# Norms and gate rows of one stage computed inside the stage before, joins by token half, modulation over seven stages

## What is computed

```python
for i in range(DEPTH):                       # 4 layers, mixers: gdn, sb, dsa, gdn
    x = x + 0.5 * swiglu(rmsnorm(x, ffn1_norm[i]), ffn1_w_gu[i], ffn1_w_down[i])
    x = x + mixer_i(rmsnorm(x, mix_norm[i]))
    x = x + 0.5 * swiglu(rmsnorm(x, ffn2_norm[i]), ffn2_w_gu[i], ffn2_w_down[i])
x = rmsnorm(x, final_norm)
...
m = split(silu(c) @ mod_w[i] + mod_b[i], 9)  # shift, scale, gate for three places
modulate(x, g, shift, scale) = rmsnorm(x, g) * (1 + scale) + shift
macaron_ffn(xs, ...) = xs + 0.5 * gate * swiglu(modulate(xs, g, shift, scale), ...)
```

## Time and profile before

| what | us |
|---|---|
| median of 3 runs | 3823.49 (3817.28 to 3826.62) |
| the profiled execution | 3812.9 |
| its span, first to last instruction | 3811.1 |
| PE busy | 3521.2 (92%) |
| DVE busy | 2263.3 (59%) |
| ACT busy | 1843.9 (48%) |
| GpSimd busy | 610.4 (16%) |
| a feed-forward stage of the first model with nothing beside it | 186.44 |

### The profile page before, as it was taken

The page is one execution under the profiler, slowest core; times in us unless marked ns, Lnnn a source line. Parts: engine busy times, 40 slices in busy tenths (PEclk is TensorE's granted clock), DMA queues, the critical chain, the costliest instruction groups (busy, mean ns, idle before and its releaser), DMA issues. The chain is left out here.

```text
span 3811.1 us, 44895 instructions
## 1 busy us (share of the span) xinstructions
PE 3521.2 (92%) x18342; PEld 2970.9 (78%) x18342; DVE 2263.3 (59%) x2508; ACT 1843.9 (48%) x2354; POOL 610.4 (16%) x208
## 2 busy tenths in 40 slices
PE   7989899999899996899999899899998799999999
PEld 6879777788788875688888778787888468787887
DVE  4566569675666667666667555545455555545654
ACT  4454356664456552456554344444443344444443
POOL 0001149571133320142401100000000000000000
PEclk9999999999999998999999999999999899999999
DMA  5532156565376752376742145454544125454453
GB/s 221 188 133 89 45 210 248 216 250 189 116 270 236 265 199 100 145 265 241 263 160 96 57 147 188 163 188 155 188 168 160 38 89 188 158 191 148 155 204 133
DMA packets 89977, 653.55 MB, mean 171 GB/s; under 512 B 10033, under 2 KB 10033, under 8 KB 10929
## 3 DMA queue, kind: packets, MB, share of 16 engines
q1 hardware_dynamic: 78768, 573.10, 41.5%
q0 software_dynamic: 11008, 77.60, 5.7%
HBM read 649.61 MB, written 1.05 MB: 171 GB/s over the span
## 5 line engine op out<-in xcount | busy, mean ns | idle before, releaser
L1562 DVE TENSOR_TENSOR w_lo<-raw,w_hi 128x2048 fp32r<-128x2048 f32 x540 | 1420.9, 2636 | 646.7 <-ACT w_hi L1080 646.4
L1080 ACT ACTIVATE w_hi<-raw 128x2048 fp32r<-128x2048 f32 x540 | 1031.2, 1913 | 592.2 <-PE acc L521 403.3
L519 PE MATMUL wrk<-w_hi,h_hi 128*128 128x512 f32 (+1 forms) x2496 | 971.2, 389 | 58.8 <-DVE w_lo L1562 37.9
L521 PE MATMUL wrk<-w_hi,h_lo 128*128 128x512 f32 (+1 forms) x2496 | 954.7, 382 | 0.0
L520 PE MATMUL wrk<-w_lo,h_hi 128*128 128x512 f32 (+1 forms) x2496 | 953.9, 382 | 0.0
L519 PEld LDWEIGHTS wrk<-w_hi,h_hi 128*128 128x128 f32 x2496 | 472.5, 189 | 155.2 <-DVE w_lo L1562 48.9
L2308 POOL TENSOR_TENSOR arena<-arena,c 128x2048 f32<-128x2048 f32 x92 | 490.7, 5342 | 472.6 <-ACT arena L1080 447.6
L521 PEld LDWEIGHTS wrk<-w_hi,h_lo 128*128 128x128 f32 x2496 | 472.2, 189 | 92.5
L520 PEld LDWEIGHTS wrk<-w_lo,h_hi 128*128 128x128 f32 x2496 | 472.8, 189 | 85.0 <-issue 0.2
L519 PE MATMUL acc<-w_hi,hid_hi 128*128 128x512 f32 x1144 | 447.4, 391 | 9.4 <-DVE hid_lo L1645 9.4
L521 PE MATMUL acc<-w_hi,hid_lo 128*128 128x512 f32 x1144 | 445.4, 389 | 0.0
(11 more groups left out here) (263 smaller groups left out, 3864.5 us busy)
## 6 DMA issues: line engine op xcount, KB each, us to landing
raw<-in_wts SPq DMA_DIRECT2D x540, 1024.0 KB, 4.8
arena<-in_mods POOLq DMA_DIRECT2D x72, 1024.0 KB, 5.2
const<-in_const SPq DMA_DIRECT2D x1, 2176.0 KB, 10.1
c<-in_bias POOLq DMA_DIRECT2D x8, 256.0 KB, 3.4
x<-in_x SPq DMA_DIRECT2D x1, 1024.0 KB, 5.3
c<-in_c SPq DMA_DIRECT2D x1, 1024.0 KB, 4.8
out<-x SPq DMA_DIRECT2D x1, 1024.0 KB, 3.9
row<-in_rows SPq DMA_DIRECT2D x1, 512.0 KB, 11.3
```

Source lines behind the costliest of these rows:

```text
L519: nc.tensor.matmul(o, l_h, r_h, start=first, stop=False, skip_group_check=True)
L521: return nc.tensor.matmul(o, l_l, r_h, start=False, stop=last, skip_group_check=True)
L1080: return nc.scalar.activation(o, i, f, **kw)
L1562: tt(w_lo[:, ns % SLOTS, :], raw[:, ns % SLOTS, :], w_hi[:, ns % SLOTS, :].bitcast(F32), ALU.subtract).then_inc(lo_ready, 1)
```

## The change

- The list of stages has `mod` inside `ffn2_3` (step 2) and `final_norm` inside `b0_ctx` (step 2): their ACT and DVE instructions are laid behind that step's.
- `AHEAD`: inside `ffn2_3`, `b0_ctx` and `b0_ffn0`, at step 4, ACT makes the statistics and DVE the normalised stream of the next stage, `b0_ctx`, `b0_ffn0` and the context part of `b0_attn` ("ready"). Each such place, and `final_norm`, has ACT load two activation tables. `stat` is doubled for it. PE turns the first two quarters of such a stage between the last `down` blocks. SP loads `c` at the start of `ffn2_3`, no longer before `b0_ctx`.
- `gate_rows` of the five feed-forward stages moves into step 6 of its own stage, `rows` into step 1 of `ffn1_0`, and again into step 1 of `ffn2_0` (the tile `c` is overwritten by `mix_0`).
- Modulation is shared by seven stages, with 14, 12, 14, 13, 13, 13 and 13 products from `ffn1_0` on.
- For a follower that needs a fresh norm ("norm"), the last `down` blocks go by token half: `turn_hid` of the last step one block earlier, both column halves of token half 0, then token half 1. Statistics and normalising of half 0 are laid beside the blocks of half 1.
- With a shift, ACT now writes the scaled and shifted quarter to `shifted` and copies it to `h_hi` in one instruction of 512 columns; DVE subtracts once.
- In the gated-delta mixer two `side` units come ahead of the wait for the squares (one in the second half), and later places have as many fewer.

The core of the diff:

```diff
+INSIDE = dict(rows="ffn2_0", mod="ffn2_3", final_norm="b0_ctx")
+AHEAD = dict(ffn2_3="b0_ctx", b0_ctx="b0_ffn0", b0_ffn0="b0_attn")
+ROWS_AT, MOD_AT, FINAL_AT, AHEAD_AT, GATE_AT = 1, 2, 2, 4, 6
+MOD_SHARE = dict(ffn1_0=7, ffn2_0=6, ffn1_1=7, ffn2_1=13, ffn1_2=13, ffn2_2=13, ffn1_3=13)
...
-                if "l" in prm:
-                    gate_rows(i, name, prm)
...
                     down(s - 1, 0, 0)
+                    if s == STEPS - 1 and not early:
+                        turn_hid(s)
                     down(s - 1, 0, 1)
                     if s == STEPS - 1:
-                        turn_hid(s)
+                        if early:
+                            turn_hid(s)
+                        else:
+                            down(s, 0, 0)
+                            down(s, 0, 1)
                     down(s - 1, 1, 0)
                     down(s - 1, 1, 1)
+                    if name in ROWS_IN and s == ROWS_AT:
+                        rows(i, name)
+                    if "l" in prm and s == GATE_AT:
+                        gate_rows(i, name, prm)
...
-                prepare(0, range(12, 16), range(16, 18), range(18, 20), range(20, 24))
+                prepare(0, range(12, 14), range(14, 17), range(17, 18), range(18, 20), range(20, 24))
...
-                prepare(1, [29], [30], [], [31])
+                prepare(1, [29], [30], [], [], [31])
...
+                    if name in AHEAD and s == AHEAD_AT:
+                        j = op_at(AHEAD[name])
+                        act.wait_ge(der_ready, 1)
+                        nc.scalar.preload_act_table_set("natural_log_exp_and_others")
+                        statistics(j, src=(c, c_new, before(j, "c")) if ops[j][0] == "attn" else None)
+                        nc.scalar.preload_act_table_set("silu_and_others")
...
-                m = fn(o, v, ACT.Copy, scale=a) if shift is None else fn(o, v, ACT.Identity, scale=a, bias=shift)
+                    if shift is None:
+                        m = fn(h_hi[:, k, tok(t)], v, ACT.Copy, scale=a)
+                    else:
+                        steps.mark(fn(shifted[:, 8 * t + k, :], v, ACT.Identity, scale=a, bias=shift))
+                if shift is not None:
+                    steps.wait()
+                    m = fn(h_hi[:, 4 * half:4 * half + 4, tok(t)], shifted[:, 8 * t + 4 * half:8 * t + 4 * half + 4, :], ACT.Copy)
```

More of the change, by code:

```diff
@@ L53, with mod_start @@
 OPS = op_list()
-MOD_OPS = ["ffn2_0", "ffn1_1", "ffn2_1", "ffn1_2", "ffn2_2", "ffn1_3"]
-MOD_PIECES = 2 * 9 * KC // 2
-MOD_EACH = MOD_PIECES // len(MOD_OPS)
+INSIDE = dict(rows="ffn2_0", mod="ffn2_3", final_norm="b0_ctx")
+AHEAD = dict(ffn2_3="b0_ctx", b0_ctx="b0_ffn0", b0_ffn0="b0_attn")
+ROWS_AT, MOD_AT, FINAL_AT, AHEAD_AT, GATE_AT = 1, 2, 2, 4, 6
+MOD_SHARE = dict(ffn1_0=7, ffn2_0=6, ffn1_1=7, ffn2_1=13, ffn1_2=13, ffn2_2=13, ffn1_3=13)
+MOD_OPS = list(MOD_SHARE)
+ROWS_IN = ("ffn1_0", "ffn2_0")
+MOD_PIECES = sum(MOD_SHARE.values())
+def mod_start(name):
+    return sum(MOD_SHARE[n] for n in MOD_OPS[:MOD_OPS.index(name)])
 CTX_CHUNKS = 5 * KC
@@ L216, in bank_uses @@
     if kind == "ffn":
-        return ["row0", "row1"] * ("l" in prm) + [f"{n}" for s in range(STEPS) for n in (f"gu{s}0", f"gu{s}1", f"t{s}")]
+        rows_at = {GATE_AT: ["row0", "row1"]} if "l" in prm else {ROWS_AT: [f"mrow{r}" for r in range(4)]} if prm["a"] in ("ffn1_norm0", "ffn2_norm0") else {}
+        return [n for s in range(STEPS) for n in [f"gu{s}0", f"gu{s}1"] + rows_at.get(s, []) + [f"t{s}"]]
     if kind == "final":
         return []
-    if kind == "rows":
-        return ["row0", "row1", "row2", "row3"]
-    if kind == "mod":
+    if kind in ("rows", "mod"):
         return []
@@ L433, in follower, with opens, op_at, stat_of @@
                 j += 1
-            ok = j < len(ops) and late(ops[j][0], ops[j][2]) and all(k not in UPDATES for k, _, _ in ops[i + 1:j])
-            return j if ok and ops[j][2]["x"] == ops[i][2]["x"] else None
+            return j if j < len(ops) else None
+        def opens(i):
+            if ops[i][1] in AHEAD.values():
+                return "ready"
+            return "late" if late(ops[i][0], ops[i][2]) else "norm"
+        def op_at(name):
+            return [k for k, o in enumerate(ops) if o[1] == name][0]
+        def stat_of(i, nth=0):
+            return stat[:, (before(i, "norm") + nth) % 2, :]
         def turned_bank(i, t, half, nth=0):
@@ L562, in turn @@
                     v = h_tok
+                    if opens(i) == "ready" and not nth:
+                        last = [k for k in range(i) if ops[k][0] in UPDATES and ops[k][1] not in INSIDE][-1]
+                        _, ready, count = stream(last)
+                        pe.wait_ge(ready, count + 2 * t + half + 1)
                 if nth:
@@ L761, in scores, with prepare @@
                     m.then_inc(filled, 1)
-                def prepare(half, first, second, third, fourth):
+                def prepare(half, ahead, first, second, third, fourth):
                     k, heads = 2 * g + half, range(half * HALF, half * HALF + HALF)
@@ L1658, in ffn @@
                         split_to(ns + 3 * s + 3)
+                    if name == "ffn2_3" and s == MOD_AT:
+                        mod()
+                    if name == "b0_ctx" and s == FINAL_AT:
+                        j = op_at("final_norm")
+                        final(j, *ops[j][1:])
+                    if name in AHEAD and s == AHEAD_AT:
+                        j = op_at(AHEAD[name])
+                        normalise(j, src=(c,) if ops[j][0] == "attn" else None)
                 hid_low(STEPS - 1)
```

239 lines of the change are left out of this document (135 added, 104 removed).

## The result

| what | before | after |
|---|---|---|
| median | 3820.39 us | 3751.11 us (3745.91 to 3754.33) |
| ratio | | 0.9823, 95% interval 0.981 to 0.9837 |
| the profiled execution | 3812.9 | 3753.37 |
| its span | 3811.1 | 3751.3 |

What follows compares the result with a forecast made beforehand. PE, busy 92% of the span, was taken as the bound, so gains lie in its idle time, non-product work and low clock. Terms sum to -75.6 us, 3823.5 to 3748 us; forecast 3738 to 3758, wider range 3728 to 3782.

Steps and rivals of the forecast that it cites:

- Modulation and rows: Feed-forward stages: sharing modulation over seven stages and moving rows inside gives -21 in ffn2_0, -3 in ffn1_1, +4.2 in ffn1_0.
- Ready openings: Boundary work moved into earlier steps: b0_ctx -15.6 us, b0_ffn0 -10.4, ffn2_3 +1.0; together -25.
- rival D: ACT is blocked by work put into the steps; insertions cost up to 3 us each, 3781 us; chance 0.12.
- b0_attn: This stage's opening: ready context quarters give -6.0 us, earlier x stream quarters -1.5; sum -7.5 (-4 to -10).
- Gated-delta mixers: mix_0 and mix_3: units ahead of the squares' wait remove idle time and low clock; -5.4 us each, -10.8 together.
- unit 16's wait: First half of a gated-delta mixer: PE waits 3.3 us again for unit 16's weight piece, which DVE lowers late.
- Rival B: Waits only move in mixers and norm openings, so 10.8 + 12.5 us are not gained; 3771 us; chance 0.2.
- Norm openings: Mixers and gated stages: subtraction leaves the opening's chain, reordered end loses 0.65; -1.3 per mixer, sum -12.5 us.
- rival C: All the idle time and the low clock behind it goes, in mixers and openings; 3730 us; chance 0.14.

Runs made afterwards that it cites:

- e10: Changed kernel with modulation back in six stages of 12 pieces, 24 products in ffn2_0, no rows in ffn1_0: 3772.75 us, 0.9884 of the kernel before.
- e2: Changed kernel with ACT's two modulation sums of a stage's last step placed behind the two silu gates: 3776.51 us, 0.989 of the kernel before.
- e5: Changed kernel with modulation sums ending at step 9, so ACT has none in the last step: 3747.44 us, 0.9808 of the kernel before.
- e11: Changed kernel with the norm openings and the stage ends ahead of them as in the kernel before: 3759.36 us, 0.9843 of the kernel before.
- e1_again: The changed kernel unedited, run and traced a second time: 3755.68 us, 0.9834 of the kernel before.
- e7: Changed kernel with unit 31 moved beside unit 30 behind the sums, in the gated-delta mixers' second half: 3743.03 us, 0.98 of the kernel before.

## Why the prediction was right, and where it was not

**What bounds the kernel** was read rightly: PE's busy time did not change, and the sum was one of idle pieces. The reading by windows against a quiet stage carried it.

**Modulation and rows**: -21.5 for -21, and PE's waits in `ffn2_0` are 0.7 us in all. The claim that DVE's slow subtractions are behind them, and that half the products would end them, is borne out by e10. The reason I gave for a part of it, ACT's four copies in the opening, is not shown: with the rows inside but 24 products the stage took 214.2, and without the wait of 4.2 that the early turn adds it would be 2.5 below the 212.5 of before; that much could be theirs. The +4.2 of `ffn1_0` was right as far as it went (+6.1 with the 1.9 of the early turn), and so was -3 in `ffn1_1` (-1.3).

**Ready openings**: -16.0, -10.6 and +0.9 for -15.6, -10.4 and +1.0. The gate rows stand in step 6 as one block of 1.95 with PE's next matmul right behind them (2511.56 and 2513.26 in `b0_ctx`), so rival D did not happen. A table load put into step 2 of `b0_ctx` (for `final_norm`), with ACT's instructions on both sides of it, has no further pause in front or behind:

```profile
2439.48 1.91 ACT L1124 ACTIVATE w_hi<-raw 128x2048 fp32r<-128x2048 f32 x1
2441.41 1.28 ACT L1258 ACT_TABLE_LOAD   x1
2442.70 1.07 ACT L1124 ACTIVATE h<-x 128x1024 f32<-128x1024 f32 x1
```

So the row's 1.28 was the right price here, and with PE idle for 0.6 and 0.8 us in these stages nothing more reached it. The Trainium skill ("ScalarE: Activation LUTs", section "What ACT_TABLE_LOAD costs") gives 2.66 us for a switch, drain included; these rows agree with its load part alone.

**`b0_attn`**: the first product starts 5.3 us after the stage before (5.7 predicted, 11.7 before), and the `x` stream's wait is 9.04 for 10.57, the predicted 1.5. The rest is 2.2 us: some 1.4 is a lower stretch behind the opening that is gone, and 0.8 comes later in the stage. In the second trace a part of that stretch is back, 1.5 of the 2.4 us by which it is longer; the other 0.9 stays open. About half of what this term gave beyond the forecast is thus luck of the clock.

**Gated-delta mixers**: the mechanism was right at each place. The sums 3.65 instead of 6.50, unit 16's wait 3.44 for 3.3. The term failed in its size, and by the clock: I took the time of the short matmuls at the scores from the earlier trace rows and its surroundings as they were, at full clock, and let DVE's chain decide the end. PE's scores and decay rows are a part of that chain, in turns with DVE. With the clock low behind the remaining pause of 3.0 us they took 13.0 for 7.1, and the mixer's end came as late as before. Where the clock stayed up, the mixer gained 6.2 of the 6.7. No run undoes the two units of the first half alone, so how the gain divides between the halves is read from the rows only. (The term's own sum is a little off: 5.58 of wait and 2.7 of clock are 8.3, not 8.4.) Rival B had the outcome for these mixers (the waits only move), not its reason.

**Norm openings**: the failed step. I priced the reordered end at 0.65, the wait for `hid_lo`. It was 2.0 in each of four stages: I had looked at what follows the turn and not at what it waits for, and so missed that ACT's sums delay the gates (e2, e5). The gain of 1.3 at the openings was there (1.5), but part of it went to lower clock behind them: `mix_1` and `mix_2` came out 0.9 and 0.7 longer, at a granted clock of 0.92 and 0.82 where it was 0.94 and 0.85. In the gated stages, where there are no sums, the term was 7.3 and 12.7 came, 6.7 of it by the openings (e11). There PE starts on the first half of the quarters before the second half is normalised, and in `b1_ffn0` the clock stays at 1.00 (0.98 in the earlier trace rows); I had given this the chain through the joins alone.

**The total** was nearer than its parts: 25 us too good in the `ffn1` stages and mixers, 5 too bad in the gated ones and 4 in the others, which leaves the 16 of the traces. Another 10 were made good because the profiled execution of before lay 7.5 us below its median and the changed kernel's 2.3 above, and 3 more because the median of before is 3820.4 with one run more, not 3823.5. That the result lies 3 us from the forecast's middle is in good part luck. Two of the forecast's bounds don't follow from its own pieces either: the good ends of the terms add up to 3729, not 3723, and rival C's pieces, as they are listed, to about 3735, not 3730.

## What to carry to other kernels

When a step is moved ahead, price what it waits for, back through every engine, and not only what waits for it: here a transpose one block earlier ran into sums that had been free. A pause is worth more in one place than in another: PE's idle time that must remain should stand ahead of another engine's long result, not in the middle of a chain in which PE's short matmuls take turns with DVE. And a stage length read from one trace near a pause of a few us holds the clock of that execution; take a second trace before a change of 5 us there is explained.

## What the runs showed of the hardware

The granted clock behind the same pause of 3.0 us, in the same program, was 0.51 in one execution and 1.00 in another, which is 6 us on a mixer; behind a wait of 2.6 us in `b0_attn` it was 1.00 in one and 0.66 in the other. The changed kernel's times spread over 8.2 us in e1_again, those of e7, where the pause is moved, over 2.4. Otherwise the two traces agree within 0.4 us a stage. DVE's subtraction beside a GpSimd product took 6.33 us in the earlier trace rows for 2.28 alone. ScalarE's table loads took 1.28 us each, with the instruction in front ending 0.02 us before and the one behind starting 0.01 us after. With 24 products in eight steps PE stood still for 16.9 us of a stage (e10, 4.2 of them at the early turn), with 12 to 14 in eight or nine steps for 0.65 to 3.3: twice the products cost far more than twice the time.
